# A hybrid decoder layer with routed experts on one core: a fixed first block for each expert, and most tiles' choice of experts made inside the mixing stage

## The reference

```python
group_p = softmax(xf @ w_rg)
g_sel = argmax(group_p + b_rg)                     # one group of 8 experts
e_p = softmax((xf @ w_re)[group g_sel])
_, e_loc = top_k(e_p + b_re[g_sel], 2)             # two experts in it
gates = group_p[g_sel] * e_w / sum(e_w)
...
h = silu(xb @ w_gate[eb]) * (xb @ w_up[eb])        # a block of 128 rows, one expert
y[tok] += (h @ w_down[eb]) * gate
```

## Time and profile before

| | us |
|---|---|
| median of 3 runs | 2676.52 |
| lowest, highest | 2675.8, 2679.08 |
| the profiled execution's own time | 2677.96 |
| its span, first to last instruction | 2675.7 |
| PE busy in the span | 2335.8 |
| DVE, ACT, POOL busy | 1028.6, 706.6, 371.8 |

### The profile page before, as it was taken

One profiled execution on the slowest core, in us unless ns is written; L12 is line 12 of the kernel. 1 busy time (PEld: TensorE's weight loads), 2 busy tenths in 40 slices (PEclk: granted clock), 3 DMA queues, 4 the chain that ended last, 5 costly groups with the idle time before them and its releaser, 6 DMA issues. The chain is left out here.

```text
span 2675.7 us, 36194 instructions
## 1 busy us (share of the span) xinstructions
PE 2335.8 (87%) x13227; PEld 1339.1 (50%) x13227; DVE 1028.6 (38%) x1696; ACT 706.6 (26%) x1820; POOL 371.8 (14%) x465
## 2 busy tenths in 40 slices
PE   5999999989948999999999999606999999999960
PEld 2444454433536666666666666404444444444430
DVE  2524325224225655355556555272111111111128
ACT  2302113012114554345445544200111111111112
POOL 1010100100201011210110010001122122212225
PEclk9999999999978999899999999858999999999985
DMA  7031030300363112121131121156999999999957
GB/s 259 24 96 67 30 125 12 115 27 11 94 191 102 55 55 71 55 80 55 55 109 55 55 86 62 43 212 268 358 355 362 361 366 358 356 357 358 361 217 304
DMA packets 174143, 440.29 MB, mean 165 GB/s; under 512 B 45250, under 2 KB 86474, under 8 KB 149402
## 3 DMA queue, kind: packets, MB, share of 16 engines
q1 hardware_dynamic: 147705, 350.80, 37.0%
q0 software_dynamic: 19152, 69.74, 6.4%
q10 hardware_dynamic: 7152, 17.91, 1.8%
HBM read 345.06 MB, written 94.83 MB: 164 GB/s over the span
## 5 line engine op out<-in xcount | busy, mean ns | idle before, releaser
L821 PE MATMUL p_ps<-p_xt,p_w 128*128 128x512 f32 x1088 | 480.5, 600 | 0.7 <-issue 0.7
L2738 PE MATMUL p_ps<-p_w_arena,p_x_arena 128*128 128x512 f32 x1024 | 444.7, 592 | 0.0
L821 PEld LDWEIGHTS p_ps<-p_xt,p_w 128*128 128x128 f32 x1088 | 206.7, 192 | 258.8 <-issue 253.2
L2738 PEld LDWEIGHTS p_ps<-p_w_arena,p_x_arena 128*128 128x128 f32 x1024 | 194.6, 190 | 244.4 <-issue 244.4
L2126 PE MATMUL p_ps<-p_w_out,p_mixt 128*128 128x512 f32 x544 | 251.7, 607 | 0.0
L2754 PE MATMUL p_ps<-p_w_arena,p_y_arena 128*128 128x512 f32 x512 | 232.6, 597 | 0.0
L2661 DVE SCALAR_TENSOR_TENSOR p_y_arena<-p_y_arena,p_ps 128x256 f32<-128x256 f32 x64 | 26.9, 421 | 462.1 <-ACT p_y_arena L2516 462.1
L2126 PEld LDWEIGHTS p_ps<-p_w_out,p_mixt 128*128 128x128 f32 x544 | 99.2, 192 | 105.3 <-issue 103.2
L830 PE MATMUL p_ps<-p_w,p_xt 128*128 128x144 f32 (+1 forms) x512 | 146.6, 439 | 0.0
L2471 POOL DMA_INDIRECT s_y<-p_y_arena,p_home x66 | 66.4, 1006 | 554.3 <-PE p_ps L2721 310.5
L2754 PEld LDWEIGHTS p_ps<-p_w_arena,p_y_arena 128*128 128x128 f32 x512 | 92.1, 190 | 94.3 <-issue 91.8
(11 more groups left out here) (358 smaller groups left out, 3168.0 us busy)
## 6 DMA issues: line engine op xcount, KB each, us to landing
p_w_arena<-in_w_exp_gate SPq DMA_DIRECT2D x64, 1024.0 KB, 8.0
p_w_arena<-in_w_exp_up SPq DMA_DIRECT2D x64, 1024.0 KB, 11.2
p_w_arena<-in_w_exp_down SPq DMA_DIRECT2D x64, 1024.0 KB, 10.1
p_x<-in_x_prompt SPq DMA_DIRECT2D x32, 512.0 KB, 4.8
p_w_arena<-s_y SPq DMA_DIRECT2D x16, 1024.0 KB, 13.3
p_w<-in_w_in SPq DMA_DIRECT2D x4, 2048.0 KB, 13.1
p_spread<-s_roots SPq DMA_DIRECT2D x16, 512.0 KB, 7.0
s_kv<-p_us SPq DMA_DIRECT2D x32, 256.0 KB, 2.3
```

The lines of the kernel that those rows point to most:

```text
L821: ins = mm(ps[:, job % 4, :], w[:, c, at:at + P], xt[s % 2][:, c, :], start=(c == 0), stop=(c == KC - 1))
L2738: t = mm(ps[:, 2 + b, :], xt[b][:, c, :], w_gu[bw][:, :, c, :], start=(c == 0), stop=(c == KC - 1))
```

## The change

Block j of the first 64 blocks now always belongs to expert j, whatever the number of its rows. Places are fixed: expert e has 17 blocks of 128 places in a new DRAM tensor `s_ids`, and row r of an expert has place r. Further blocks of an expert with over 128 rows come behind the 64.

- The choice for tiles 0 to 12 is made in three groups (5, 5 and 3 tiles) inside the mixing loop. DVE has the choice itself, in five pieces at three places of two iterations per group; ACT an exponential and a copy of the counts; PE the function `earlier` behind the logits of iterations 9, 12 and 15; POOL, at the top of iterations 10, 13 and 16, the weights (`weigh_rows`) and places (`place_rows`), and then 26 indirect transfers of 128 numbers each to `s_ids`, each waiting for the one before. The logits stay in SBUF.
- The route stage chooses for the last four tiles only. The first 64 blocks' lists come from `s_ids` plus eight products of one-hot matrices for these four tiles. Weights of the first four blocks are requested at once, since the block's number is the expert's. POOL writes the two empty blocks before it waits for `slots`, then gathers four blocks, then sends the last four tiles' eight lists to `s_ids`, and only then enters the loop.
- In the expert stage, the gather runs four blocks ahead. For the last eight gathers (`gather_listed`) POOL loads the list itself from `s_ids` and makes slot and home in a chain of seven small operations. The load of h moves from the route stage to behind the last weights.
- `project_in` clears `s_ids` with nine transfers.

```diff
+PLACES = TILES
+SPILL = 48
+HOMES = TILES * P
+GROUPS = [(0, 5), (5, 10), (10, 13), (13, 17)]
...
+            ids = S["ids"].rearrange("r c -> (r c)").rearrange("(p n) -> p n", p=P)
+            for n in range(9):
+                sp.dma_start(ids[:, 121 * n:121 * (n + 1)], zero[:, 0:121]).then_inc(on["misc_out"], 16)
...
+def earlier(mm, out, c, upto, ones):
+
+    n = c.n
+    both = c.both.rearrange("p t e -> p (t e)")
+    mm(out[:, 0:(n + 1) * NE], upto[:], both, start=True, stop=False)
+    for d in range(1, n + 1):
+        ins = mm(out[:, d * NE:(n + 1) * NE], ones[:], both[:, 0:(n + 1 - d) * NE], start=False, stop=(d == n))
+    return ins
...
+        GROUP_AT, EXPERTS_AT, COUNT_AT, PLACE_AT = {8: 0, 11: 1, 14: 2}, {9: 0, 12: 1, 15: 2}, {8: 0, 11: 1, 14: 2}, {
+            10: 0, 13: 1, 16: 2}
+        SEND_AT = {10: (0, 0, 5), 11: (0, 5, 10), 13: (1, 0, 5), 14: (1, 5, 10), 16: (2, 0, 6)}
...
+            def place_rows(g):
+                c = choices[g]
+                pool.wait_ge(on["counted"], g + 1)
+                base = K["base"][:] if g else c.const("base0")
+                own(nc.gpsimd.tensor_tensor(rank[:, 0:c.n + 1, :], rank[:, 0:c.n + 1, :], bc(base, [P, c.n + 1, NE], 1), ALU.add))
+                own(nc.gpsimd.tensor_copy(K["base"][:], rank[:, c.n, :]))
+                own(nc.gpsimd.tensor_tensor(c.chosen, c.chosen, bc(rank[:, 0:c.n, :], [P, c.n, 2, NE], 2), ALU.mult))
+                size = NE
+                while size > 2:
+                    size //= 2
+                    own(nc.gpsimd.tensor_tensor(c.chosen[:, :, :, 0:size], c.chosen[:, :, :, 0:size],
+                                                c.chosen[:, :, :, size:2 * size], ALU.add))
...
+                    pool.wait_ge(K["ids_out"], 16 * (2 * lo + n))
+                    pool.indirect_dma_start(out=S["ids"].rearrange("r (c u) -> (r c) u", u=1),
+                                            out_offset=bass.IndirectOffsetOnAxis(ap=place_i[0:r, t, k:k + 1], axis=0),
+                                            in_=route[0:r, at:at + 1], in_offset=None).then_inc(K["ids_out"], 16)
...
+                if t in PLACE_AT:
+                    weigh_rows(PLACE_AT[t])
+                    place_rows(PLACE_AT[t])
+                if t in SEND_AT:
+                    send_rows(*SEND_AT[t])
...
-                nc.scalar.copy(lg[:], ps[:, 7, 0:NR]).then_inc(lg_ready.sem, 1)
-                lg_ready.after(act, t)
-                r = n_rows(t)
-                act.dma_start(rows(S["logits"], data(t), r), lg[0:r]).then_inc(lg_out.sem, 16)
...
+                    nc.scalar.copy(keys_flat[:, 0:size], ps[:, 7, P:P + size]).then_inc(on["counted"], 1)
+                nc.scalar.copy(lg_of(t), ps[:, 7, 0:NR]).then_inc(lg_ready.sem, 1)
...
                 denominators(t)
+                if t in GROUP_AT:
+                    shift_logits(GROUP_AT[t])
+                if t in EXPERTS_AT:
+                    picks[EXPERTS_AT[t]].pick_first()
...
                 turned_probabilities(t, 3)
+                if t in GROUP_AT:
+                    dve.wait_ge(on["exps"], GROUP_AT[t] + 1)
+                    picks[GROUP_AT[t]].pick_group()
+                if t in EXPERTS_AT:
+                    count_experts(EXPERTS_AT[t])
...
                     level_update(t + 1, 4)
+                if t in GROUP_AT:
+                    picks[GROUP_AT[t]].score_experts()
...
-            sp.dma_start(h_all[:, 0:NT, :], S["h"][0:SEQ].rearrange("(n p) d -> p n d", p=P)).then_inc(on["h_in"], 16)
-            sp.dma_start(h_all[0:NS, NT, :], S["h"][SEQ:NTOK]).then_inc(on["h_in"], 16)
-
-            sp.wait_ge(on["owner_ready"], 1)
...
-            def load_weights(j, b):
-                e = sp.value_load(owner[0:1, bass.ds(j, 1)], min_val=0, max_val=NE - 1)
+            def load_weights(j, e, b):
...
+            with sp.Fori(0, NE - R, R) as i:
                 for b in ring:
-                    load_weights(i + b, b)
+                    load_weights(i + b, i + b, b)
+            total = n_blocks(sp)
+            with sp.Fori(NE - R, total, R) as i:
...
+            sp.wait_ge(K["ids_out"], 16 * 2 * TILES)
+            sp.dma_start(h_all[:, 0:NT, :], S["h"][0:SEQ].rearrange("(n p) d -> p n d", p=P)).then_inc(on["h_in"], 16)
...
+            def gather_listed(j, b, arrived):
+                n = b % 2
+                q = pool.value_load(owner[0:1, bass.ds(2 * (j + (R - NE)) + 1, 1)], min_val=0, max_val=NE * PLACES)
+                pool.wait_ge(turned.sem, turned.back(j, R))
+                apart(pool, on["slots_ready"], 1)
+                with nc.allow_non_contiguous_dma(reason="one row to one column"):
+                    pool.dma_start(raw[n][:], S["ids"][bass.ds(q, 1)].rearrange("o c -> c o")).then_inc(raw_in[n], 16)
+                pool.wait_ge(raw_in[n], arrived)
...
             for b in two:
                 send(b)
                 pool.wait_ge(y_out[b], 16)
-            for j in range(3):
+            pool.wait_ge(on["slots_ready"], 1)
+            for j in range(R):
                 gather(j, j)
-            with pool.Fori(0, total, R) as i:
+            pool.wait_ge(on["placed"], 1)
+            for n in range(2 * n3):
+                pool.wait_ge(K["ids_out"], 16 * (2 * LAST[0] + n))
...
+            pool.wait_ge(K["ids_out"], 16 * 2 * TILES)
+            with pool.Fori(0, NE - 2 * R, R) as i:
                 for b in ring:
-                    gather(i + b + 3, (b + 3) % R)
+                    gather(i + b + R, b)
                     scatter(i + b, b % 2, 8 * i + 16 * (b // 2) + 16, 8 * i + 16 * ((b + 1) // 2) + 16)
+            total = n_blocks(pool)
+            with pool.Fori(NE - 2 * R, total, R) as i:
+                for b in ring:
+                    gather_listed(i + b + R, b, 8 * (i + (2 * R - NE)) + 16 * (b // 2) + 16)
```

More of the change, by code:

```diff
@@ L993, in bc, with __init__, cut, const @@
     return ap.unsqueeze(axis).to_broadcast(shape)
-def mix_prompt(nc, A, S, O):
+class Choice:
+    def __init__(self, n, ex, sums, tops, small, vec, oh, big, both, bias, route):
+        def cut(t, lo, shape):
+            ap = t[:, lo:lo + math.prod(shape)]
+            if len(shape) == 2:
+                return ap.rearrange("p (a b) -> p a b", a=shape[0])
+            if len(shape) == 3:
+                return ap.rearrange("p (a b c) -> p a b c", a=shape[0], b=shape[1])
+            return ap
+        self.n = n
+        self.ex = cut(ex, 0, (n, NG + 1, EPG))
+        self.sums, self.tops = sums[:, 0:n], cut(tops, 0, (n, NG + 1))
+        self.top, self.group_w, self.total = (small[:, k * n:(k + 1) * n] for k in range(3))
+        self.cand, self.score, self.group, self.probs = (cut(vec, k * n * NG, (n, NG)) for k in range(4))
+        self.picks = cut(oh, 0, (n, 2, EPG))
+        self.picked = cut(oh, 2 * n * EPG, (n, 2, EPG))
+        self.terms = cut(big, 0, (n, NG, EPG))
+        self.chosen = cut(big, 0, (n, 2, NE))
+        self.both = cut(both, 0, (n + 1, NE))
+        self.bias, self.route = bias, route
+    def const(self, name):
+        return self.route[:, ROUTE[name]]
@@ L1035, in mix_prompt @@
         zs = [sb(f"zs{b}", [P, H, HD]) for b in two]
-        th = [sb(f"th{b}", [P, H, HD]) for b in two]
+        th = sb("th", [P, H, HD])
         x = sb("x", [P, D])
@@ new lines, in moe @@
+        ident, w = K["ident"], K["w"]
+        work = h_all[:].rearrange("p t d -> p (t d)")
+        upto, ones, route = work[:, 6 * D:6 * D + P], work[:, 6 * D + P:6 * D + 2 * P], work[:, 7 * D:7 * D + ROUTE_ALL]
+        bias = work[:, 8 * D:8 * D + NR]
+        last = Choice(n3, work[:, 0:288], work[:, 288:292], work[:, 292:328], work[:, 328:340], work[:, 340:468], work[:, 468:596],
+                   work[:, 596:1108], work[:, 1108:1428], bias, route)
+        rank = cut(work, 1428, (n3 + 1, NE))
@@ new lines, in moe @@
+        at_lane, at_block = cut(work, 1748, (n3, 2, P)), cut(work, 2772, (n3, 2, NE))
+        picked = cut(work, 3284, (n3, 2, NE))
+        lists = work[0:NE, 3796:3796 + P]
+        place_f, room_f, lane_f = (cut(work, 3924 + 2 * n3 * k, (n3, 2)) for k in range(3))
+        listed, none, token = (cut(work, 3948 + k * NE, (NE,)) for k in range(3))
+        over = cut(work, 4140, (NE, PLACES - 1))
+        extra, upto0, upto1, under = (cut(work, 5164 + k * NE, (NE,)) for k in range(4))
+        cum = [upto0, upto1]
@@ L2353, in moe, with const @@
+        who, gone, count_f, spare_c = (work[:, 5420 + k:5421 + k] for k in range(4))
+        def const(name):
+            return route[:, ROUTE[name]]
+        place_i = sb("place_i", [P, n3, 2], I32)
+        owner_c, total_c = sb("owner_c", [P, 2], I32), sb("total_c", [P, 1], I32)
+        owner = sb("owner", [1, 2 * SPILL + 1], I32)
+        slots, homes = sb("slots", [P, NE], I32), sb("homes", [P, SLOTS], I32)
         slot = [sb(f"slot{b}", [P, 1], I32) for b in ring]
+        raw = [sb(f"raw{b}", [P, 1]) for b in two]
@@ L2601, in _, with invert, reduced @@
```

(34 more changed lines are left out.)

501 lines of the change are left out of this document (315 added, 186 removed).

## The result

| | before | after |
|---|---|---|
| median, us | 2677.80 | 2639.93 |
| lowest to highest, us | 2675.8 to 2681.64 (4 runs) | 2632.95 to 2645.29 (4 runs) |
| span of the profiled execution, us | 2675.7 | 2643.5 |

The ratio is 0.9862, 95% interval 0.9842 to 0.9882: the change makes the kernel 37 us faster. The forecast was 2645, with 2618 to 2672 as its range. The profiled execution of after is the slowest of its four (2645.29), so its span is some 5 us above what the median stands for.

The account below looks back on a forecast made before the run. PE bounds mixing; PE and DMA are both nearly full in the expert stage; in the route stage PE waits on a chain. -59.4 + 7 + 7 - 6 + 20 = -31.4, giving 2645 us, range 2618 to 2672.

Parts of the forecast that it names:

- Route stage, -59.4: Between mixing and the first gate product: earlier start -7.1, shorter chain to `slots` -47.1, no spare scatters -10.5, loaded gather +5.3.
- Mixing, +7: Mixing stage: PE's `earlier` products +6.1, leftovers of DVE and ACT +1, POOL's added work 0.
- Start of the loop, +7: Start of the expert loop: POOL's eight list writes delay block 4's gather, so PE stalls; bounds 0 and +50.
- the threshold of 22.5 us: Start of the expert loop: no PE stall if POOL enters within 22.5 us of the first product.
- One block further ahead, -6: Expert stage: a longer gather lead removes most of PE's 7.9 us of waits for gathered rows; bounds -7.9, 0.
- Last blocks, +20: Last eight blocks: POOL's list load and chain make 16.0 us per block against PE's 11.7, for some five blocks.
- The bound of +37: Upper bound of the last eight blocks' term, with all eight list loads in loaded queues.
- the load of h fits: 0: End of the expert stage: h's 8.65 MB fit into 104 GB/s spare over 87 us, costing 0.
- both paybacks hidden: Rival: lists land quickly at the expert loop's start and end, +5 together instead of +7 and +20; 2623 us, chance 0.2.
- Slow list writes: Rival: at the expert loop's start each list write takes 6.7 us, +30 instead of +7; 2668 us, chance 0.12.
- Exposed mixing: Rival: DVE's and POOL's added work falls on the mixing path, 61 us instead of 7; 2699 us, chance 0.07.
- a second sum: Start of the expert loop: at about 2.0 us per transfer eight writes take 16 us, term 0, time 2638.

Follow-up runs that it names:

- the bare run: Changed kernel with the choice for tiles 0 to 12 and its 26 list writes left out of the mixing stage; 2630.94 us, ratio 0.9826.
- the doubled writes: Changed kernel with the eight list writes between the first four gathers and POOL's loop made twice; 2661.66 us, ratio 0.9932.
- the held-back weights: Changed kernel: lists only from block 64, asked early; three constants after keys; h in pieces; weights of blocks 2 and 3 wait for first gather; 2624.84 us.
- the run with the constants behind the keys: Changed kernel with three loads of constants moved behind tile 8's keys and values on SP's queue; 2633.87 us, ratio 0.984.
- the run with lists late: Changed kernel with lists loaded only for blocks from 64 on, two loads behind earlier scatters, two behind the last; 2630.67 us, ratio 0.9825.

## Why the prediction was right, step by step

- **Route stage, -59.4.** Measured -59.2 (-6.9, -46.8, -5.5), and by the waits that were named, so this is no luck. Costing each operation by the earlier trace rows for 4 tiles gave 23.7 us to `slots`, the profile has 24.05. The first gather took 8.5 us from issue to PE's first turn, the +5.3 for loaded queues was a little too much, and POOL's first copy a little longer than thought (below).
- **Mixing, +7: the term was mis-sized.** It measured +13.8. The step that failed is that only `earlier` and leftovers of DVE are paid. The iterations with `earlier` grew by 7.2, not 6.1. Its products in iteration 9 are busy 0.86 + 1.85 us:

```profile
1356.18 0.86 PE L1124 MATMUL p_ps<-p_kct,p_upto 128*128 128x384 f32 x2
1356.88 1.85 PE L1126 MATMUL p_ps<-p_kct,p_ones 128*128 128x320 f32 x10
```

  The leftovers measured 2.2 against the bare run, and 2.7 between the profiles of before and after, not 1; which engine leaves them was not followed. And 3.8 are three loads of constants that the prediction did not look at: it counted what SP has less to do in the route stage, and not where those loads had gone. Iterations grew by 2.8, 2.8 and 1.6 where 2.4, 2.4 and 1.2 were forecast, and by 3.8 in one where nothing was forecast. The whole term is 13.8, near the 15 us that the prediction named as a sign of being wrong.
- **Start of the loop, +7: it measured 0.** The step that failed is the threshold of 22.5 us. Entry was forecast at 24 to 36 us after the first product and was 27.2, within that. But PE asked for block 4's rows after 37.7 us, not 32.7: its second pair began 23.8 us after the first (23.3 forecast), and that pair's gate and up products took 13.90 us, where the prediction added 9.4. Those 9.4 are what is left of a pair of 23.3 us without its gate and up products, the wrong part of it; in the kernel before they took 13.90 as well. With 37.7 in the place of 32.7 the prediction's own sum, at 3.3 us a write, would have given no stall. That there is a threshold is shown by the doubled writes and by the held-back weights.
- **One block further ahead, -6.** In the kernel before, alone, it gave 0.3% (0.13 to 0.46), some 8 us by the ratio and 6.6 in the stretch to the last weights; in the changed kernel that stretch is 6.6 shorter too.
- **Last blocks, +20.** Measured +16.5, and shown to be the list loads by the run without them. POOL's loop took 16.2, 17.6, 13.3, 14.1 and 13.6 us between scatters while the queues were full, 15.0 on average where 16 was forecast, and 11.5, 9.3 and 9.3 after that. Counted as the prediction counts, five blocks at 3.3 us over PE's 11.7 make 16.5. POOL waited 5.7 to 10.8 us for each of the first five lists, less than the 9.3 taken but for one, and from the list to the gather's issue it took 2.8 us (2506.42 to 2509.21), not 4.7. The bound of +37 does not follow from its own terms: eight blocks at 16.0 make 34, at 10.2 for the list 42. Three of the scatters:

```profile
2497.23 1.03 POOL L2762 DMA_INDIRECT s_y<-p_y_arena,p_home  x1 [0.80 <-POOL p_home L2753]
2511.34 1.03 POOL L2762 DMA_INDIRECT s_y<-p_y_arena,p_home  x1 [0.85 <-POOL p_home L2753]
2524.91 1.03 POOL L2762 DMA_INDIRECT s_y<-p_y_arena,p_home  x1 [0.80 <-POOL p_home L2753]
```

  "A late gather or scatter reaches PE" is half of it. PE's one long wait there, its last product, and the last product of the kernel before:

```profile
2516.90 1.96 PE L2997 MATMUL p_ps<-k_ident,p_x_arena 128*128 128x128 f32 x8 [7.54 <-DMA p_x_arena<-s_hn,p_slot]
2542.16 3.70 PE L3026 MATMUL p_ps<-p_w_arena,p_y_arena 128*128 128x512 f32 x8
2582.71 3.70 PE L2754 MATMUL p_ps<-p_w_arena,p_y_arena 128*128 128x512 f32 x8
```

  From the request for the last weights to the end of these products it took 55.0 us, before 46.0: 9.0 more, of which 7.5 are the wait and the rest slower products right behind it. The other 7.5 of the 16.5 never reached PE. The last scatter began 9.1 us after PE's end, before 1.6, since POOL still had to work off its own list loads, the last four of them for blocks behind the 64 that these inputs do not have.

  That "the load of h fits: 0" was half right. It took no bandwidth that PE's transfers needed, but it lengthened the list loads that POOL stood waiting for: 9 or 10 of the 16.5.
- **The rivals.** Of "both paybacks hidden" the first half came true, the second did not. Slow list writes did not happen: in the changed kernel they were 2.4 to 7.6 us apart, 4.2 on average. Exposed mixing is refused: the bare run gained 7.7 us (9.1 in the stage), not 60. The 0.857 us operations of the last stage told nothing about mixing, where such an operation still took 0.20 us in the changed kernel.

For the start of the loop the prediction had a second sum, by the figure of the Trainium skill's page "DMA: Bandwidth & Descriptors". Its estimate was 2638 with a term of 0, which is what came, but by luck: it had eight writes of 2.0 us, 16 in all, and they took 33.7 (1791.73 to 1825.39), more than my 26. What made the term 0 was PE's later need. In mixing, where the queues are nearly empty (a DMA share of 0.01 from 1360 to 1376), writes followed one another like this:

```profile
1369.12 0.97 POOL L1496 DMA_INDIRECT s_ids<-p_s_keys,p_place_i  x1 [1.45 <-DMA s_ids<-p_s_keys,p_place_i]
1371.50 0.96 POOL L1496 DMA_INDIRECT s_ids<-p_s_keys,p_place_i  x1 [1.42 <-DMA s_ids<-p_s_keys,p_place_i]
1373.89 0.96 POOL L1496 DMA_INDIRECT s_ids<-p_s_keys,p_place_i  x1 [1.43 <-DMA s_ids<-p_s_keys,p_place_i]
```

One each 2.4 us, where I had taken 3.3. The Trainium skill's page "DMA: Bandwidth & Descriptors", section "Anatomy of one DMA — SWDGE (gpsimd) path", has a fixed part of about 2.0 us for each; this trace agrees roughly for empty queues (2.4), and not for full ones, where a write took up to 7.6 us, and 13.7 behind the held-back weights.

## What to carry to other kernels

Where work moves out of a stage, follow the loads that it needs to their new place and ask what stands behind them in that queue: three small transfers ahead of the one that the bound engine needed cost 2.4 us of wait here, and 1.5 of lower clock behind it. Where an engine issues a transfer and waits for it before its next duty, price the landing at the load of the queues in that stretch, and count who else loads them; asking early and using late takes it off the path. Ask too where an engine that is late ends: half of what the list loads cost came after PE was done. And try a lead of one more buffer alone: it gave a fifth of what the large restructuring did.

## What the runs showed of the hardware that was not expected

**The same instructions at two clocks.** Around the sample tile, windows of the kernel before, and of the run with the constants behind the keys, in which this stretch has the same work:

```profile
1022.60:1141.40 118.80, 111.20 (x1038) 77.84 (x1037) 54.48 (x94) 43.55 (x118) 22.95 (x17) 0.90 0.18 54
1020.00:1030.00 10.00, 10.00 (x72) 9.06 (x73) 2.81 (x7) 1.84 (x6) 0.00 (x0) 0.60 0.05 17
```

```profile
1022.80:1135.40 112.60, 104.66 (x1034) 72.78 (x1033) 54.35 (x94) 43.28 (x117) 22.95 (x17) 0.95 0.20 57
1020.00:1030.00 10.00, 9.96 (x97) 8.56 (x97) 5.32 (x10) 2.30 (x8) 0.00 (x0) 1.00 0.02 8
```

The third number from the end is the granted clock: 0.60 against 1.00 in the same ten microseconds, 6.2 us over the stretch. From 1025 to 1030 it is 0.50, the level of 1.2 GHz, in the one, and 1.00, that of 2.4 GHz, in the other. PE had done the same before it in both, busy 18.5 of the 20 us from 1000 to 1020. Of the 13 profiles eight have the slower form, the kernel before and after among them, and five the faster: the run with lists late and all four with the constants behind the keys. That edit stands behind this stretch, and lists late is without it, so it is no cause that one can see, but with these counts it isn't excluded. This is about the size of the spread between executions, and a difference of 6 us between two single profiles is no evidence for an edit. What decides between the two was not found.

**POOL's copy as long as DVE's instruction.** POOL's first copy of slots took over five times its usual 0.20 us; beside it in the timeline of the changed kernel:

```profile
1782.55 1.22 DVE L2902 TENSOR_TENSOR p_h_all<-p_h_all 128x1024 f32<-128x1024 f32 x1
1782.69 1.12 POOL L2711 COPY p_slot<-p_slots 128x1 int32<-128x1 int32 x1 [11.28 <-DVE p_slots L2899]
```

It ended at 1783.81, when DVE's had ended at 1783.77; DVE's has two inputs in SBUF. The copy took 1.11 to 1.13 us in all eleven profiles of the changed kernel and its variants, and 0.18 in the kernel before, where DVE was done. The Trainium skill's page "SBUF — State Buffer", section "Who interferes with whom", says that a DVE instruction with two SBUF inputs contends with a GpSimd instruction that reads SBUF, and calls the contention an exclusive lock; the two ends agree with it. It cost 0.9 us on the path to the first gather, and no experiment here separated it.
